# Two written-out layers, an opening made inside the first feed-forward, and other beginnings of three stages in a two-part transformer kernel

## The reference, cut to what matters

```
cos, sin = rope_tables(positions)
for l in range(2):
    x = x + 0.5 * swiglu(rms_norm(x, ffn1_norm[l]), ffn1_w_in[l], ffn1_w_out[l])
    ... fox, rwkv and moba mixers of rms_norm(x, mix_norm[l]) @ mix_w_in[l]; moba uses cos, sin
    x = x + memory_cross_attention(rms_norm(x, ...), rms_norm(mem, xattn_mem_norm[l]), ...)
    x = x + 0.5 * swiglu(rms_norm(x, ffn2_norm[l]), ffn2_w_in[l], ffn2_w_out[l])
```

```
hx = modulate(rms_norm_2(x), sh1, sc1)
hc = modulate(rms_norm_2(ctx), csh1, csc1)
... both through w_in: attention over context and latents, and a gated delta rule (conv, scans)
x = x + g1 * merge_branches(attn_x, gdn_x, gate_x, w_pa, w_pd, w_out)
x = x + g2 * conv_ffn(modulate(rms_norm_2(x), sh2, sc2), w_up, ffn_conv_w, ffn_conv_b, w_down)
```

## Time and profile before

| | |
|---|---|
| median of 3 runs | 2724.61 us (2722.59 to 2729.61) |
| the profiled execution | 2729.99 us, span 2728.2 us |
| mean granted TensorE clock | 0.906 of 2.4 GHz |
| TensorE busy | 2393.3 us (88%), 18119 products |
| GpSimd / ScalarE / VectorE busy | 1210.6 / 1128.3 / 1064.2 us |
| moved by DMA | 305.97 MB |

### The profile page before, as it was taken

One profiled execution on the slowest core, in us unless ns is written; L12 is line 12 of the kernel. 1 busy time (PEld: TensorE's weight loads), 2 busy tenths in 40 slices (PEclk: granted clock), 3 DMA queues, 4 the chain that ended last, 5 costly groups with the idle time before them and its releaser, 6 DMA issues. The chain is left out here.

```text
span 2728.2 us, 42768 instructions
## 1 busy us (share of the span) xinstructions
PE 2393.3 (88%) x18119; PEld 2081.0 (76%) x18119; DVE 1064.2 (39%) x2109; ACT 1128.3 (41%) x1531; POOL 1210.6 (44%) x308
## 2 busy tenths in 40 slices
PE   5998988997998998988988999698976876897998
PEld 4997945486998998865557899576845666896997
DVE  2212754233220220756232321257756666423550
ACT  5433432354542543333145443455863323343442
POOL 2874600062875875520034678233300001574784
PEclk8999977987999999987978999899977777998999
DMA  4654511331653654511233354332100001453552
GB/s 149 201 174 120 166 39 40 124 124 63 196 183 123 196 182 139 155 62 47 93 121 111 125 185 155 105 96 62 47 1 1 2 1 45 131 166 114 166 178 99
DMA packets 298690, 305.97 MB, mean 112 GB/s; under 512 B 7249, under 2 KB 294461, under 8 KB 298493
## 3 DMA queue, kind: packets, MB, share of 16 engines
q1 hardware_dynamic: 298493, 303.16, 34.7%
HBM read 302.09 MB, written 1.05 MB: 111 GB/s over the span
## 5 line engine op out<-in xcount | busy, mean ns | idle before, releaser
L369 POOL TENSOR_TENSOR slab_lo<-ring,slab_hi 128x2048 fp32r<-128x2048 f32 (+1 forms) x242 | 1092.5, 4527 | 874.3 <-ACT slab_hi L358 874.3
L358 ACT CAST slab_hi<-ring 128x2048 fp32r<-128x2048 f32 (+1 forms) x242 | 451.4, 1870 | 619.1 <-PE bank L403 281.6
L434 PE MATMUL bank<-ffn_h_hi,slab_hi 128*128 128x256 f32 x1344 | 330.7, 284 | 0.0
L435 PE MATMUL bank<-ffn_h_lo,slab_hi 128*128 128x256 f32 x1344 | 329.7, 283 | 0.0
L435 PEld LDWEIGHTS bank<-ffn_h_lo,slab_hi 128*128 128x128 f32 x1344 | 258.0, 192 | 0.1
L434 PEld LDWEIGHTS bank<-ffn_h_hi,slab_hi 128*128 128x128 f32 x1344 | 257.9, 192 | 0.1
L1480 POOL TENSOR_TENSOR inv_m<-inv_d,const 128x512 f32<-128x512 f32 x24 | 30.3, 1266 | 423.5 <-ACT inv_d L1538 318.7
L401 PE MATMUL bank<-ffn_hidden_hi,slab_hi 128*128 128x256 f32 x704 | 199.2, 283 | 0.0
L402 PE MATMUL bank<-ffn_hidden_lo,slab_hi 128*128 128x256 f32 x704 | 199.2, 283 | 0.0
L403 PE MATMUL bank<-ffn_hidden_hi,slab_lo 128*128 128x256 f32 x704 | 199.2, 283 | 0.0
L439 PE MATMUL bank<-ffn_h_hi,slab_lo 128*128 128x256 f32 x1344 | 189.1, 283 | 4.5 <-POOL slab_lo L369 4.4
(11 more groups left out here) (613 smaller groups left out, 5823.9 us busy)
## 6 DMA issues: line engine op xcount, KB each, us to landing
ring<-in_ffn_w_in SPq DMA_DIRECT2D x88, 1024.0 KB, 5.1
ring<-in_ffn_w_out SPq DMA_DIRECT2D x32, 1024.0 KB, 5.0
ring<-in_w_in SPq DMA_DIRECT2D x30, 1024.0 KB, 5.4
ring<-in_mix_w_in SPq DMA_DIRECT2D x24, 1024.0 KB, 5.4
ring<-in_w_mod SPq DMA_DIRECT2D x24, 1024.0 KB, 5.2
ring<-in_w_up SPq DMA_DIRECT2D x22, 1024.0 KB, 5.1
ring<-in_ffn_w_out SPq DMA_DIRECT2D x16, 768.0 KB, 4.4
ring<-in_mix_w_out SPq DMA_DIRECT2D x8, 1024.0 KB, 5.2
```

Of the source, the lines that this page charges most:

```text
L358: act.copy(self.hi[i % self.PLACES][:, 0:w], K.ring[n % RING][:, 0:w]).then_inc(self.hi_ready, 1)
L369: pool.tensor_tensor(self.lo[i % self.PLACES][:, 0:w], place[:, 0:w], self.hi[i % self.PLACES][:, 0:w].bitcast(F32), ALU.subtract).then_in ...
L434: pe.matmul(out, w[0][:, k, col], act[0][:, k, :], start=(k == 0), stop=False)
L435: pe.matmul(out, w[0][:, k, col], act[1][:, k, :], start=False, stop=False)
```

## The change

- The loop over the layers is written out. `K.restart()` at a layer's end stays, the one before the first layer goes.
- `prologue` keeps x, the first table of constants and eight rows of the first layer's gain. It issues the first three slabs and behind them memory, the second table and the positions. It has no memory norm, no sine and no parameters of the second block.
- A new class `Opening` puts these into the first layer's first feed-forward, one part behind each of its steps on TensorE, ScalarE and VectorE: memory's turning behind steps 1 to 4, the sum over its squares behind 5, its scaling behind 6, the angles behind 7, sine and cosine behind 8, the second block's parameters behind 9, both layers' parameters behind 10. All in PSUM bank 7. The small DMAs stand between the slabs' DMAs. Layer 2's begin has no parameters to load.
- `inputs_stage` goes; its work is done by `SecondInputs` at the begin of the latent stage. The latents are normed and split first; units 0 to 7, which need only them, start before the context's parts, which are made behind unit 1. `K.h` keeps the latents without their shift, and the shift is added where high and low parts are made (`shifted_hi`, `shifted_lo`), here and in the merge.
- In `merge_stage` GpSimd waits, in addition, until the four heads are scaled (`scan.scaled`), and the squares and sums for the convolution's norm are made between its last slabs.
- In `conv_ffn_stage` the norm is `ShiftedNorm` (root, scaling into PSUM banks, shift with the parts), and its first two slabs are eaten together, pair by pair (`two_slabs_first`).

The diff's core (of `Opening`, `SecondInputs` and `ShiftedNorm` the parts that order the work):

```diff
             @block.sync
             def _(sync):
-                if params is not None:
-                    params.sync_first(sync)
-                K.load_slabs(sync, n0 + RING)
-                if params is not None:
-                    params.sync(sync)
+                if opening is not None:
+                    for i in range(9):
+                        K.load_slabs(sync, n0 + RING + 1 + i)
+                        opening.sync_rows(sync, i)
                 K.load_slabs(sync, n0 + FK + 12 + RING)
+                if opening is not None:
+                    opening.sync_end(sync)
...
+                    if opening is not None:
+                        opening.pe(pe, i)
                 pe.wait_ge(product_ready, N - 1)
                 ffn_out_pe(K, pe, split, hidden, x_updated, lambda: pe.wait_ge(product_ready, N))
...
+                        if opening is not None:
+                            opening.dve(dve, i)
...
+class Opening:
...
+    MEM, SUM, ROOT, ANGLES, SINES, ROWS2, PARAMS = 1, 5, 6, 7, 8, 9, 10
...
+        sync.dma_start(self.mem_rows[:, :, :], K.a["mem"][0].rearrange("(t p) d -> p t d", p=P)).then_inc(self.mem_arrived, 16)
+        sync.dma_start(K.consts[1][:, :], K.a["consts1"]).then_inc(self.consts1_in, 16)
+        sync.dma_start(self.pos_i[:, :], K.a["positions"]).then_inc(self.pos_in, 16)
...
+    def sync_rows(self, sync, i):
+
+        if i == 0:
+            sync.wait_ge(self.rows2.cleared, 1)
+            for dst, src in self.rows2.pieces:
+                sync.dma_start(dst, src).then_inc(self.rows2.arrived, 16)
+        elif i == 1:
+            sync.wait_ge(self.cleared, 1)
+        if 1 <= i <= 8:
+            for p in self.params:
+                for dst, src in p.pieces[(i - 1) * 4:i * 4]:
+                    sync.dma_start(dst, src).then_inc(self.arrived, 16)
...
+    def pe(self, pe, i):
+        K = self.K
+        if self.MEM <= i < self.SUM:
+            g = i - self.MEM
+            pe.wait_ge(self.mem_arrived, 16)
+            if g:
+                pe.wait_ge(self.copied, g)
+            for j in range(2):
+                for t in range(TT):
+                    last = pe.transpose(self.bank[:, j * T + t * P:j * T + (t + 1) * P],
+                                        self.mem_rows[:, t, (2 * g + j) * P:(2 * g + j + 1) * P], K.c("ident"))
+            last.then_inc(self.turned, 1)
+        elif i == self.SUM:
+            pe.wait_ge(self.copied, 4)
+            for k in range(KD):
+                if k % 2 == 0:
+                    pe.wait_ge(self.squared, k // 2 + 1)
+                last = pe.matmul(self.low, K.c("ones"), K.mem[:, k, :], start=(k == 0), stop=(k == KD - 1))
+            last.then_inc(self.summed, 1)
+        elif i == self.ANGLES:
+            pe.wait_ge(self.pos_ready, 1)
+            pe.wait_ge(self.mem_ready, 1)
+            pe.matmul(self.low, K.c("ones", slice(0, 1)), self.pos[:, :], start=True, stop=True).then_inc(self.pos_spread, 1)
+        elif i == self.ROWS2:
+            pe.wait_ge(self.angles_ready, 2)
+            self.rows2.pe(pe)
+        elif i == self.PARAMS:
+            pe.wait_ge(self.rows2.prm_ready, 1)
+            pe.wait_ge(self.arrived, 16 * sum(len(p.pieces) for p in self.params))
+            for l, p in enumerate(self.params):
+                last = pe.transpose(self.bank[:, l * P:(l + 1) * P], p.rows[:, :], K.c("ident"))
+            last.then_inc(self.prm_turned, 1)
...
+    def act(self, act, i):
+        K = self.K
+        if self.MEM <= i < self.SUM:
...
+            act.wait_ge(self.turned, i - self.MEM + 1)
+            act.copy(self.mem_in[:, g, :].rearrange("p a t -> p (a t)"), self.bank[:, :]).then_inc(self.copied, 1)
+            act.wait_ge(self.copied, i - self.MEM + 1)
+            act.activation(K.mem[:, g, :], self.mem_in[:, g, :], ACT.Square).then_inc(self.squared, 1)
+        elif i == self.SUM:
+            act.wait_ge(self.summed, 1)
+            K.act_own.after(act, act.activation(self.high, self.low, ACT.Ln, bias=K.c("eps"), scale=1.0 / D))
+            act.activation(self.high, self.high, ACT.Exp, scale=-0.5).then_inc(self.root, 1)
+        elif i == self.SINES:
+            act.wait_ge(self.angles_ready, 1)
+            act.activation(K.sin[:, :], self.low, ACT.Sin)
+            act.activation(K.cos[:, :], self.quarter[:, :], ACT.Sin).then_inc(self.angles_ready, 1)
+        elif i == self.ROWS2:
+            self.rows2.act(act)
...
+    def dve(self, dve, i):
+        K, own, low, high = self.K, self.K.dve_own, self.low, self.high
+        if i == self.ROOT:
+            dve.wait_ge(self.root, 1)
...
+            for g in range(4):
+                last = dve.tensor_tensor(K.mem[:, pair_of(g), :], self.mem_in[:, pair_of(g), :], rstd, ALU.mult)
+            last.then_inc(self.mem_ready, 1)
+            dve.wait_ge(self.pos_in, 16)
+            dve.tensor_copy(self.pos[:, :], self.pos_i[:, :]).then_inc(self.pos_ready, 1)
+        elif i == self.ANGLES:
+            turns, quarter = self.turns[:, :], self.quarter[:, :]
+            dve.wait_ge(self.consts1_in, 16)
+            dve.wait_ge(self.pos_spread, 1)
...
+            own.after(dve, dve.tensor_scalar(turns, turns, 12582912.0, None, ALU.subtract))
...
+            own.after(dve, dve.tensor_scalar(quarter, quarter, 3.1415925, -3.1415925, ALU.min, ALU.max))
...
+def prologue(K, opening):
...
+            @block.sync
+            def _(sync):
+                sync.dma_start(K.consts[0][:, :], a["consts0"]).then_inc(first.consts_in, 16)
+                x_start(sync)
+                sync.dma_start(first.first_rows[:, :], a["ffn1_norm"][0:1, :].rearrange("a (r c) -> (a r) c", c=P))\
+                    .then_inc(first.first_in, 16)
+                K.load_slabs(sync, RING)
+                opening.sync_inputs(sync)
...
+            @block.tensor
+            def _(pe):
+                pe.wait_ge(first.consts_in, 16)
+                pe.wait_ge(first.first_in, 16)
+                pe.transpose(K.bank[6][:, 0:KD], first.first_rows[:, :], K.c("ident", slice(0, KD), n=KD))\
+                    .then_inc(first.first_turned, 1)
+                x_pe(pe)
...
+    def pe(self, pe):
+        self.pe_sum(pe, 0)
+        self.ctx_pe(pe)
+        self.pe_sum(pe, 1)
...
+    def act_first(self, act):
+        self.act_squares(act, 0)
+        self.act_root(act, 0)
+        self.ctx_act(act)
+        act.wait_ge(self.ctx_copied, 4)
+        self.act_squares(act, 1)
+
+    def act_latent_parts(self, act):
+        for t in range(4):
+            act.wait_ge(self.h_ready[0], t + 1)
+            shifted_hi(act, self.parts[0], t, self.K.h[:, pair_of(t), :], self.shift[0])
+
+    def act_ctx_parts(self, act):
+        for t in range(4):
+            act.wait_ge(self.h_ready[1], t + 1)
+            shifted_hi(act, self.parts[1], t, self.places[t], self.shift[1])
...
+        for t in range(5):
+            if t < 4:
+                for k in (2 * t, 2 * t + 1):
+                    last = dve.scalar_tensor_tensor(K.h[:, k, :], K.x[:, k, :], gains[:, 0, k:k + 1], self.rstd[0][:, :],
+                                                    ALU.mult, ALU.mult)
+                last.then_inc(self.h_ready[0], 1)
+            if t:
+                shifted_lo(dve, self.parts[0], t - 1, K.h[:, pair_of(t - 1), :], self.shift[0])
...
+        unit_bank = lambda u: K.bank[u % 4 if u < 8 else u % 8]
...
             def _(sync):
+                inputs.sync(sync)
                 K.load_slabs(sync, n0 + SLABS)
+                sync.wait_ge(inputs.consts_in, 16)
...
+                pool.wait_ge(inputs.parts[0].lo_ready, 4)
                 split.pool(pool)
...
+                inputs.pe(pe)
+                pe.wait_ge(inputs.consts_in, 16)
                 for u in range(prep.FIRST):
-                    if u >= 8:
-                        pe.wait_ge(z_ready, u - 7)
-                    split.pe(pe, u, K.bank[u % 8], T if u < 8 else 2 * T)
+                    if u >= 4:
+                        pe.wait_ge(z_ready, u - 3 if u < 12 else 8)
+                    if u == 8:
+                        pe.wait_ge(inputs.parts[1].lo_ready, 4)
+                    split.pe(pe, u, unit_bank(u), T if u < 8 else 2 * T,
+                             first=(lambda k: pe.wait_ge(inputs.parts[0].lo_ready, k // 2 + 1)) if u == 0 else None)
...
+                inputs.act_first(act)
+                act.wait_ge(inputs.consts_in, 16)
                 split.act(act, 0)
+                inputs.act_latent_parts(act)
                 split.act(act, 1)
+                inputs.act_root(act, 1)
                 for u in range(prep.FIRST):
                     split.wait(act, u)
                     split.act(act, u + 2)
-                    b = K.bank[u % 8]
+                    b = unit_bank(u)
+                    if u == 1:
...
+                inputs.dve_latents(dve)
                 prep.dve_first(dve)
+                dve.wait_ge(inputs.consts_in, 16)
+                inputs.dve_ctx(dve)
...
```

(31 more changed lines are left out.)

390 lines of the change are left out of this document (212 added, 178 removed).

## The result

The changed kernel takes **2685.89 us** (median of 5 runs, 2684.34 to 2691.41) against 2728.52 us for the kernel before in the same comparison (5 runs). The ratio is 0.9846, 95% interval 0.9832 to 0.986: 42.6 us faster. 2676 us were forecast, with a range of 2661 to 2697, and a gain of 48.9 us.

The account below looks back on a forecast made before the run. TensorE, busy 88% of the span, was taken as the bound, with gains where stages begin. 28.3 - 7.6 + 4.2 + 12 + 5 + 7 = 48.9 us off the median 2724.6 gave 2676 us, range 2661 to 2697.

Parts of the forecast that it names:

- the opening's two chains: Start of the first feed-forward: VectorE's scalings with first low part, or ScalarE's slab cast with first pair; 4 us.
- 1. The opening: First feed-forward: first product at 17 us instead of 45.26, gain 28.3 us; the moved work costs 7.6 us inside.
- the 0.5 for waits at the seams: First feed-forward: 0.5 us added to the opening's cost for TensorE's waits at seven seams.
- Rival D: First feed-forward: ScalarE's opening work delays slab casts and starves TensorE; 2730 us if all ten steps lose 5.4; chance 0.02.
- my signs of being wrong: TensorE waiting for slab_hi or slab_lo in the first feed-forward, or layer 2's first slab still 4 us behind.
- 2. The second layer: Layer 2's begin: without the jump back and the queued DMAs the first slab comes earlier; gain 4.2 us, bounds 1 and 5.
- 3. The latent stage: Latent stage's begin: latents first, first product at 1733, unit 4 waits 2.8 us; gain 12 us, bounds 5 and 18.7.
- the microsecond kept back for 1.2 GHz: Latent stage's begin: one us held back from the gain for a spell of TensorE at the lower clock.
- 4. The merge: Merge's begin: GpSimd's wait brings the first product 6.8 us earlier, part lost to a later block; gain 5 us, bounds 0 and 8.
- The rule that I had set against this part: Merge's begin: VectorE and GpSimd lock a shared port pair, so the block moves to the next steps rather than goes.
- 5. The convolution: Convolution's begin: sums between the merge's last slabs, first product after 14.5 instead of 21.2 us; gain 7 us, bounds 4 and 9.
- Rival B: Later begins give gains back through GpSimd's lock, ScalarE's order, a DMA-only layer gain and 1.2 GHz; 2696 us, chance 0.22.

Follow-up runs that it names:

- the casts' edit: The changed kernel with ScalarE's eight context casts one pair behind each of latent units 1 to 4 instead of all behind unit 1: ratio 0.9807, 2675.32 us.
- the largest edit behind the opening: The changed kernel with GpSimd also holding the merge's slabs 2 to 5 until the state step two slabs earlier has its gdk: ratio 0.9823, 2677.56 us.

## Why the prediction was right, and where it was not

**The side and the range held** because the largest term was read from rows that do not change: the opening's two chains gave 17 us for the first product (16.13), and what enters a feed-forward costs TensorE's own time. That the sum came within 4.8 us of the span's gain is partly luck. Against the forecast the merge lacks 5.7 us, the latent stage 3.1, layer 2's first feed-forward 2.2 and the rest of layer 2 1.9. The opening with its feed-forward brought 3.5 us more, the convolution 2.2 more, and the final norm 1.4 that nobody forecast; the kernel with nothing but its layers written out has these 1.4 us too (20.41).

**1. The opening.** 28.3 - 7.6 were forecast, 29.1 - 4.9 came. The cost inside was 6.3 us by the feed-forward without it, against 7.1 for the instructions; the 0.5 for waits at the seams was not there. The other 1.4 us of the difference is a spell at 1.2 GHz that the first feed-forward of the kernel before had (its first 39 us have a clock of 0.96), and that I had not counted. Rival D never came near: four times the squares did not move the end. Of my signs of being wrong one appeared in name, the wait of 1.1 us for `slab_lo` in the first feed-forward, but the kernel before has it as well.

**2. The second layer.** The mechanism was right: 3.6 us at the jump, 0.9 at what was queued behind it. The prediction saw the jump only as time without a releaser; at the branch itself the trace has 3.65 us on TensorE's sequencer and 3.42 us on VectorE where it is taken, and 0.08 and 0.11 where it is not. The Trainium skill (Runtime: NRT & Kernel Launch, Instruction fetch mechanics) says that a taken branch to a page outside the window makes the engine fetch that page first. The trace agrees, with these numbers, but does not show the fetch itself. What failed is that the first product's gain was taken for the layer's. When a chain in front of TensorE gets shorter the warming products start earlier with it, and here they started 5.3 us ahead of the slab's cast (849.73 against 854.99) instead of 4.15 (880.20 against 884.35) and, partly at the full clock, took 4.51 us instead of 5.49, so 1.9 us of idleness became 4.0 and the clock fell. In other executions it was 4.1 to 5.7 us, and the price 0.8 to 2.2 us against the 192.98 of the kernel before. With six warming products it came back.

**3. The latent stage.** 12 us forecast, 8.9 measured. The first product (15.65 us behind the squares) and the gap before unit 4 (3.08) were as worked out. The term that was mis-sized is the microsecond kept back for 1.2 GHz: unit 4 alone lost 2.4, units 0, 1 and 5 about 1.8 together against the forecast.

**4. The merge.** 5 us forecast, -0.7 measured; this is the step that failed. I had the block go on to the next steps "of up to 4.5 us, of which TensorE's own work hides half". There were two: of the four multiplications the first took 4.32 us, until slab 2's low part was done, and the last 4.56 us, until slab 3's was. Nothing was hidden, since TensorE needs `gdk` at once (7.13 us of waiting). Part of the -0.7 is not the wait's: without it the merge is 1.6 us longer than before. I put that down to the sums between its slabs and the longer low parts; it was not taken apart. The rule that I had set against this part would have given 0, and was right. The Trainium skill (SBUF — State Buffer, Who interferes with whom) says that where a VectorE instruction uses the port pair that it shares with GpSimd, whichever issues first has the pair for its whole instruction, and the other one is blocked. The trace agrees: VectorE's instructions from SBUF to SBUF at 0.27 to 0.29 us stood for as long as GpSimd's instruction still ran, up to 4.56 us, and those with PSUM did not.

**5. The convolution.** 7 forecast, 9.2 measured. I put the price of the three sums that stand between the merge's slabs (2.8 us) into this stage; it lies in the merge. Without it my sum is 11.7 us, and 11.9 came. Merge and convolution together were forecast at 12 and gave 8.5, and what is missing is the merge's block.

Rival B, gains given back at later begins, was thus right in one of its mechanisms, the lock, and had another, the clock, at the wrong begin: not the first feed-forward, but layer 2's. ScalarE's order cost what the forecast had for it (3.08 us against 2.8) and not the 7 us more of rival B, and layer 2's begin gained 4.5 us and not 1.

## What to carry to other kernels

Work that stands ahead of a bound engine's first instruction is worth most where it can be hidden inside that engine's next long stage; it costs there what it puts on the bound engine. Loading the operands early while the rest still stood ahead won nothing here. A wait that protects small instructions from an engine they share a port with has to hold at every place where they come, or the block only moves: pace the long instructions by the short ones. And when the chain in front of a product gets shorter, check what TensorE does meanwhile: idle stretches of 3 to 6 us cost 0.9 to 2.7 us behind them. Read the stage behind a mended one too: the casts' edit won 6 us up to the gates and gave 2.6 back before the merge.

## What the runs showed of the hardware that was not expected

- GpSimd's instructions behind each other do not starve VectorE, but each costs it one instruction: of four multiplications of some 0.28 us each, one was blocked by slab 2's low part (4.32 us) and one by slab 3's (4.56 us), 9.19 us together.
- A loop's branch that jumps back held TensorE's sequencer for 3.65 us and VectorE for 3.42 us; the same branch not taken cost 0.08 and 0.11 us.
- The granted clock of stretches in which TensorE works in short pieces differs between executions of the same instructions: one stage of some 630 us took 625.60 to 634.96 us, the other 628.83 to 643.41. Most of what one execution of this kernel differs from another lies there. That is about as much as the largest edit behind the opening is worth (10.35 us), so these can be judged only stage by stage.
- Behind 1.12, 1.38 and 1.91 us of idleness TensorE's first products came at the full clock; behind 2.63, 3.08, 4.01 and 5.96 us they came at 1.2 GHz. Behind 2.42 us, in the first feed-forward of the kernel before, the first came at the full clock and those from 1.4 us later at 1.2 GHz for some 3 us. The price does not follow the idle time: layer 2's first feed-forward took 195.20 us behind 4.01 us, 193.81 behind 4.06 and 194.12 behind 5.67.
